# Ten ring slots and 17 expert places for the weight loads of a two-model transformer kernel, with all transfers issued by SyncE and ScalarE

## The reference, cut to what matters

```python
def first_block(x, c, ctx, ...):
    for i in range(2):
        mod_x = (silu(c) @ w_ada[i] + b_ada[i])          # "ada": 1024 x 6144
        hx = rms_norm(x) * (1 + sc1) + sh1
        zx = hx @ w_in[i]; mx = concat(attention, pool_mix, fourier_mix)
        x = x + ga1 * (mx @ w_out[i])
        x = x + ga2 * swiglu(fx, w_gate_up[i], w_down[i])
        # the same for ctx in layer 0
# second model: zx = h @ w_in_2 (attention q k v, mLSTM q k v o, gates), @ w_out_2,
# router over 32 experts, top 2 of one group; each expert: (silu(h @ w1) * (h @ w3)) @ w2
# final rms_norm with norm_f_g_2
```

## Time and profile before

| | before |
|---|---|
| median of 3 runs | 1637.65 us (1637.15 to 1637.92) |
| the profiled execution | 1636.89 us, span 1635.1 us |
| mean granted TensorE clock | 0.93 |
| busy: TensorE / VectorE / ScalarE / GpSimd | 87% / 39% / 32% / 5% of the span |
| DMA | 395 MB, mean 242 GB/s |
| chain that ended last | PE 67%, DMA 22% (of it `R<-in_w_dram` 20%, `R<-in_w_ada_dram` 1%) |
| 192 expert loads | 1024 KB each, median 23.0 us from issue to landing |

### The profile page before, as it was taken

The page is one execution under the profiler, slowest core; times in us unless marked ns, Lnnn a source line. Parts: engine busy times, 40 slices in busy tenths (PEclk is TensorE's granted clock), DMA queues, the critical chain, the costliest instruction groups (busy, mean ns, idle before and its releaser), DMA issues.

```text
span 1635.1 us, 24940 instructions
## 1 busy us (share of the span) xinstructions
PE 1427.8 (87%) x10475; PEld 1057.2 (65%) x10476; DVE 639.6 (39%) x1232; ACT 523.6 (32%) x975; POOL 74.2 (5%) x80
## 2 busy tenths in 40 slices
PE   5998999999999999989999999998886766677565
PEld 3654476888888886847999989898643333333232
DVE  3336445333333344565655666576421111110111
ACT  4425524322122324554544454564310000000001
POOL 2000022000000012002000010000000000000000
PEclk9999999999999999999999999999897787777777
DMA  9874952613421332766656447335899999999995
GB/s 361 338 267 169 283 195 88 190 53 122 154 65 56 97 108 100 282 204 212 216 179 210 143 173 233 97 110 200 346 417 417 418 417 417 418 418 417 417 417 238
DMA packets 165244, 395.06 MB, mean 242 GB/s; under 512 B 8244, under 2 KB 121448, under 8 KB 139272
## 3 DMA queue, kind: packets, MB, share of 16 engines
q1 hardware_dynamic: 163480, 390.56, 64.9%
q0 software_dynamic: 1216, 2.21, 0.4%
q10 hardware_dynamic: 432, 0.63, 0.1%
HBM read 392.32 MB, written 1.05 MB: 241 GB/s over the span
## 4 chain that ended last, share of the span: by engine, by line
PE 67%; DMA 22%; ACT 4%; DVE 4%; issue 2%; POOL 0%; SPq 0%; DVEq 0%; ACTq 0%; POOLq 0%
DMA R<-in_w_dram 20%; PE ps L901 14%; PE ps L907 14%; PE ps L902 14%; PE ps L2734 3%; PE ps L601 3%; PE ps L923 2%; PE ps L924 2%; PE ps L929 2%; PE ps L2783 2%; PE ps L2812 1%; PE ps L1217 1%; PE ps L1274 1%; DMA R<-in_w_ada_dram 1%; PE ps L1248 1%
## 5 line engine op out<-in xcount | busy, mean ns | idle before, releaser
L870 DVE TENSOR_TENSOR WL<-R,WH 128x1024 fp32r<-128x1024 f32 (+1 forms) x202 | 226.4, 1134 | 206.6 <-ACT WH L860 206.6
L2734 PE MATMUL ps<-R,XG 128*32 128x256 f32 x2048 | 180.8, 513 | 127.4 <-DMA R<-in_w_dram 120.5
L901 PE MATMUL ps<-HH,WH 128*128 128x256 f32 (+2 forms) x872 | 273.0, 335 | 0.3 <-ACT WH L860 0.3
L902 PE MATMUL ps<-HL,WH 128*128 128x256 f32 (+2 forms) x872 | 270.3, 330 | 0.0
L860 ACT ACTIVATE WH<-R 128x1024 fp32r<-128x1024 f32 (+1 forms) x202 | 191.2, 961 | 150.5 <-PE ps L907 113.2
L2734 PEld LDWEIGHTS ps<-R,XG 128*32 128x32 f32 x2048 | 90.4, 139 | 210.5 <-issue 196.0
L901 PEld LDWEIGHTS ps<-HH,WH 128*128 128x128 f32 (+1 forms) x872 | 164.3, 188 | 23.7 <-issue 6.5
L902 PEld LDWEIGHTS ps<-HL,WH 128*128 128x128 f32 (+1 forms) x872 | 164.9, 189 | 16.7
L907 PE MATMUL ps<-HH,WL 128*128 128x256 f32 (+2 forms) x872 | 164.7, 331 | 0.0
L901 PE MATMUL ps<-GH,WH 128*128 128x512 f32 (+1 forms) x480 | 153.7, 339 | 0.1
L902 PE MATMUL ps<-GL,WH 128*128 128x512 f32 (+1 forms) x480 | 153.5, 339 | 0.0
(11 more groups left out here) (494 smaller groups left out, 1739.8 us busy)
## 6 DMA issues: line engine op xcount, KB each, us to landing
R<-in_w_dram SPq DMA_DIRECT2D x192, 1024.0 KB, 23.0
R<-in_w_ada_dram SPq DMA_DIRECT2D x72, 1024.0 KB, 6.7
R<-in_w_gate_up_dram SPq DMA_DIRECT2D x40, 1024.0 KB, 7.5
R<-in_w_in_dram SPq DMA_DIRECT2D x20, 1024.0 KB, 9.2
R<-in_w_down_dram SPq DMA_DIRECT2D x16, 768.0 KB, 4.5
R<-in_w_down_dram SPq DMA_DIRECT2D x16, 640.0 KB, 4.4
R<-in_w_in_dram SPq DMA_DIRECT2D x8, 512.0 KB, 9.4
R<-in_w_out_dram SPq DMA_DIRECT2D x16, 256.0 KB, 4.3
```

Of the source, the lines that this page charges most:

```text
L870: last = e.tensor_tensor(L, w, H.bitcast(F32), ALU.subtract)
L901: e.matmul(b[0:n, 0:N], H[:, k, 0:n], xh(k, N), start=(k == 0), stop=False)
L902: e.matmul(b[0:n, 0:N], H[:, k, 0:n], xl(k, N), start=False, stop=False)
L2734: mm = e.matmul(PS[4][32 * g:32 * g + 32, 0:256], x[:, 4 * hf + k, :], w[g // 2][:, k, 256 * (g % 2):256 * (g % 2) + 256], start=(hf == 0 ...
```

## The change

The software queue's ring shrinks from 16 KB to 128 bytes, and GpSimd issues no transfers any more. The room gives the weight ring two slots more (`SLOTS` 10), behind the split buffers, and lets three expert places instead of two lie in the area of `WPF`, `SC` and the split buffers; there are 8 further places, of which one is used once, so 17 take part in the turn. SyncE issues what GpSimd issued, at fixed points of its load order; ScalarE issues `RES` at the start and `TWO` at the head of `act_second`.

```diff
-BASE = 16512
-SLOTS = 8
+SCRATCH = 128
+BASE = 128 + SCRATCH
+SLOTS = 10
...
+    def slot_at(k):
+        return oR + 8 * KB * k if k < 8 else oW + 22 * KB + 8 * KB * (k - 8)
+
+    R = [at(f"R{i}", [128, 2048], F32, slot_at(i)) for i in range(SLOTS)]
...
-    WR = at("WR", [128, 8, 36], F32, oZ + 16 * KB)
-    RB = at("RB", [128, 36], F32, oZ + 16 * KB + 1152)
+    WR = at("WR", [128, 8, 36], F32, o2 + 22240)
+    RB = at("RB", [128, 36], F32, o2 + 23392)
...
     def act_start(e):
+        e.dma_start(RES[:, 0:S_COS], A["k_res"][:, 0:S_COS]).then_inc(d_res, 16)
         load_vectors(e, 0)
...
+    def sp_rotary_table(e):
+        e.wait_ge(s_xt, 8)
+        e.dma_start(RES[:, S_COS:S_END], A["k_res"][:, S_COS:S_END]).then_inc(d_cs, 16)
+        e.wait_ge(s_init, 2)
+
+    def sp_mixer_weights(e, layer):
+        if layer:
             e.wait_ge(s_mx, 20)
...
+    def sp_positions(e):
         e.wait_ge(s_mx, 30)
...
+    def sp_router_weights(e):
         e.wait_ge(s_mm, first_of["in2"])
-        e.dma_start(TWO[:, :], A["k_two"]).then_inc(d_two, 16)
+        for c0, n, wn, bn in ((0, 4, "w_rg_2", "b_rg_2"), (4, 32, "w_re_2", "b_re_2")):
+            e.dma_start(WR[:, :, c0:c0 + n], A[wn][0].rearrange("(k p) n -> p k n", p=128)).then_inc(d_wr, 16)
+            e.dma_start(RB[:, c0:c0 + n], A[bn][0].partition_broadcast(128)).then_inc(d_wr, 16)
...
     def act_second(e):
         act_split(e, first_of["in2"] + 1)
+        e.wait_ge(s_mm, first_of["in2"])
+        e.dma_start(TWO[:, :], A["k_two"]).then_inc(d_two2, 16)
         act_rstd(e, 4, 256, 4)
...
-    MORE = ((o2 + 8320, (s_mld, 24)), (oW, (s_mm, N_TILES)), (oW + 8 * KB, (s_mm, N_TILES)), (oH + 8 * KB, (s_mm, N_TILES)),
+    MORE = ((o2 + 8320, (s_mld, 24)), *((oS + 6816 + 8 * KB * q, (s_mm, N_TILES)) for q in range(3)), (oH + 8 * KB, (s_mm, N_TILES)),
             (oG, (s_mm, N_TILES)), (oX, (s_rtp, 4)), (oX + 8 * KB, (s_rtp, 5)))
-    ONCE = 3
+    ONCE = 4
...
+    first_top = latest[SLOTS + 1]
...
+    def sp_final_gain(e):
         e.wait_ge(s_mm, N_TILES)
         e.dma_start(NFB[:, :], A["norm_f_g_2"].partition_broadcast(128)).then_inc(d_nf, 16)
...
             for load in ring.loads[2:]:
+                if load is ring.loads[16]:
+                    sp_rotary_table(e)
+                    sp_mixer_weights(e, 0)
+                elif load is tiles[first_of["gu", 0, 0] + 10].parts[0][0]:
+                    sp_mixer_weights(e, 1)
+                elif load is tiles[first_of["gu", 1, 0] + 10].parts[0][0]:
+                    sp_positions(e)
+                elif load is tiles[first_of["in2"] + 5].parts[0][0]:
+                    sp_router_weights(e)
+                elif load is first_top:
+                    sp_final_gain(e)
                 if load.fill is not None and load.after is not None:
                     e.wait_ge(*load.after.used)
```

More of the change, by code:

```diff
@@ L174, in block_program @@
     GL = at("GL", [128, HALF, 512], F32R, oG + 22 * KB)
-    R = [at(f"R{i}", [128, 2048], F32, oR + 8 * KB * i) for i in range(SLOTS)]
+    def slot_at(k):
+        return oR + 8 * KB * k if k < 8 else oW + 22 * KB + 8 * KB * (k - 8)
+    R = [at(f"R{i}", [128, 2048], F32, slot_at(i)) for i in range(SLOTS)]
     WH = [at(f"WH{i}", [128, HALF, 128], F32R, oW + i * 11264) for i in range(2)]
@@ L186, in block_program @@
     SG = at("SG", [128, 8, 2], F32, oS + 6528)
-    WPF = at("WPF", [128, 4, 128], F32, oS + 6592)
-    ST = at("ST", [128, 48], F32, oS + 8640)
-    EB = at("EB", [128, 8], F32, oS + 8832)
+    WPF = at("WPF", [128, 4, 128], F32, oS + 6816)
+    ST = at("ST", [128, 48], F32, oS + 6592)
+    EB = at("EB", [128, 8], F32, oS + 6784)
     SC = at("SC", [128, KT, 32], F32, oS + 8864)
@@ L281, in block_program @@
     d_ring = [sem(f"d_ring{k}") for k in range(SLOTS)]
-    d_cs = sem("d_cs")
+    d_cs, d_two2 = sem("d_cs"), sem("d_two2")
     d_res, d_vec, d_wp, d_two, d_wr, d_out = (sem(n) for n in ("d_res", "d_vec", "d_wp", "d_two", "d_wr", "d_out"))
@@ L798, in held @@
     def held(tag, load):
-        return [at(f"{tag}{x}", [128, 8, 128], F32R, oR + 8 * KB * load.slot + 4 * KB * y) for y, x in enumerate("HL")]
+        return [at(f"{tag}{x}", [128, 8, 128], F32R, slot_at(load.slot) + 4 * KB * y) for y, x in enumerate("HL")]
     OUT2_ROOMS = [held("WQ", fourth)] + [[at(f"WO{j}{x}", [128, 8, 128], F32R, oH + 8 * KB * j + 4 * KB * y)
@@ L1849, in pe_rotary2 @@
         e.wait_ge(s_evi, 20 + 4 + m + 1)
-        e.wait_ge(d_two, 80)
+        e.wait_ge(d_two2, 16)
         if m >= 2:
@@ L2352, in block_program @@
     GSB, PM = small(6, 4), small(N_BLOCKS)
-    TJ = at("TJ", [128, 2, N_EXTRA, 32], F32, oW + 16 * KB)
+    TJ = at("TJ", [128, 2, N_EXTRA, 32], F32, oZ + 16 * KB)
     iota = TWO[:, B_IOTA:B_IOTA + 256]
@@ L2432, in pool_router @@
         e.wait_ge(s_m2l, 8)
-        for c0, n, wn, bn in ((0, 4, "w_rg_2", "b_rg_2"), (4, 32, "w_re_2", "b_re_2")):
-            e.dma_start(WR[:, :, c0:c0 + n], A[wn][0].rearrange("(k p) n -> p k n", p=128)).then_inc(d_wr, 16)
-            e.dma_start(RB[:, c0:c0 + n], A[bn][0].partition_broadcast(128)).then_inc(d_wr, 16)
         e.memset(ZERO[:, :], 0.0).then_inc(s_zero, 1)
+    def sp_final_gain(e):
         e.wait_ge(s_mm, N_TILES)
@@ L3061, in _ @@
         def _(e):
-            pool_mixer_weights(e, 0)
             pool_norm(e, 0, lambda k: MOD[:, 0, k, 1:2])
-            pool_mixer_weights(e, 1)
             pool_sums(e, 1, 512)
@@ L3069, in _ @@
             pool_sums(e, 3, 256)
-            pool_second(e)
+            pool_sums(e, 4, 256)
             pool_squares_a(e)
@@ L3093, in _ @@
             e.wait_ge(d_wp, 256)
-            e.wait_ge(d_two, 80)
+            e.wait_ge(d_two, 64)
+            e.wait_ge(d_two2, 16)
             e.wait_ge(d_wr, 64)
@@ L3109 @@
     from concourse.bass_utils import run_bass_kernel_spmd as _run
-    nc = _bacc.Bacc("TRN2", target_bir_lowering=False, num_devices=1)
+    nc = _bacc.Bacc("TRN2", target_bir_lowering=False, num_devices=1, dynamic_dma_scratch_size=SCRATCH)
     arrays, args = {}, {}
```

2 lines of the change are left out of this document (removed).

## The result

The changed kernel takes 1617.37 us (median of 4 runs, 1617.06 to 1619.09), against 1637.4 (1636.16 to 1637.92) for the kernel before in the same comparison: a ratio of 0.9874, 95% interval 0.9855 to 0.9893, or 20.0 us. The forecast was 1626.7 with a range down to 1622.5. The direction was right.

A forecast was written before the change was run, and what follows sets the result against it. The prediction took the expert stage as bound by DMA, its 192 loads of 1 MB; A 1.5 + B 3.7 - D 0.3 + C 6.0 = 10.9 us, off 1637.65, gave 1626.7 us, range 1622.5 to 1631.5.

The forecast's parts named there:

- gain C: Refill at the expert stage's start: three more load places bring the end forward 6.0 us (floor 4.5, ceiling 7.6).
- 173 loads at 2.53 us: Expert stage after the 19th load: remaining loads keep the old interval, so 1175.0 becomes 1613.0, against 1619.0 before.
- Start (A): Kernel start: eight ada loads issued in one go, small transfers later; eighth lands 1.5 us earlier (0.9 to 1.9).
- The rival that the order buys nothing: Kernel start: the new load order gains nought, time 1628.2 us; chance 0.08.
- in2 stall (B): Second model's in2 stage: wait for `ka0` goes, 2.2 us idle plus 1.5 lower clock, 3.7 in all (2.2 to 4.0).
- Rival 2: in2 stage: `ka0` waits for the router weights' short rows, or another engine holds tile 5; 1630.4 us, chance 0.13.
- `TWO` on ScalarE (D): Second model's norm: issuing `TWO` before ScalarE's table load costs 0.3 us, nothing if hidden, 0.6 if not.
- Rival 1: Expert refill: the added places buy nothing and only lengthen the queue; 1632.7 us, chance 0.07.
- The steady rate: Expert stage: load interval taken as unchanged; its error, half a per cent of 446 us (2 us), partly in the range.
- the loads still come at 2.53 us: Expert stage, sign expected in the profile after: the interval between load landings stays as before.
- the prediction is wrong if the steady rate differs: Expert stage, stated sign of failure: a changed rate of the steady run of loads would refute the forecast.

## Why the prediction was right or wrong

The bound was right, and so was the reading of each stage. What failed is one sentence behind gain C: "173 loads at 2.53 us".

- **Start (A), 1.5 forecast, 0.7 seen.** The landing moved by 1.4 and, with the small transfers put first again, back by 1.5: as to the landing, this term is confirmed. (Part of it is the place again: from the first to the eighth ada landing it took 17.51 with eight slots at the old offset and 17.13 at the new one, both with the small transfers late.) In the profiled execution 0.7 of it went to a lower clock in the matmuls behind it, 3.11 us for the twelve instead of 1.86. The sum had no term for that; the clock went the other way at the end, 1.4 us better. How much of A reaches TensorE varies by execution: at 980 us the kernels with B and with C taken back, whose program is the same up to that stage, are 1.9 and 0.5 ahead of before, the changed kernel 0.7, and the two with eight slots 1.4 and 1.6. The rival that the order buys nothing (1628.2) is out by the landings. The new issuer shows no gain in the steady run, as far as the runs go: the interval is 2.533 with GpSimd's transfers in the kernel (before) and without them (eight slots, old offset). No run changed the issuer and left the order. Order and issuer are two things, and the forecast counted the order alone.
- **in2 stall (B), 3.7 forecast, 3.9 seen**, and 3.7 gone when it is taken back alone. `ka0` landed at 979.73 where the forecast had 983, so the cover in front of ScalarE's split was about 6 us and not 4. The router weights cost what was put on them: issued from 969.31 to 970.85, the last landed at 977.05, 7.7 after the first issue (forecast 7); their rows are of 16 and 128 bytes, not up to 144. Rival 2 (the stall moves, 0.13) did not happen here, but with eight slots it did, at 3.2 us, so it was a fair rival.
- **`TWO` on ScalarE (D), 0.3 forecast, 0 seen.** It is issued beside the split.
- **Three places (C), 6.0 forecast, 6.7 seen to the 19th load**, 7.2 when taken back alone (6.6 of it behind the experts' first matmul). The forecast put the 19th at 1175.0 less the 4.9 of A, B and D, 1170.1; it landed at 1169.44. (By its own figures the sum gives 5.8 and not 6.0 there, 1180.84 - 1175.0.) The loads before the 19th come at the faster rate too, some ten of them in a row from the ninth on, which is 0.3 of the difference by that count. The rest lies in where the account cuts: from `N_TILES`, 5.4 ahead, the refill is 6.0. Rival 1 is out: without the three places the hole and most of the 7 us are back.
- **The steady rate, 0 forecast, 5.0 seen.** This is the step that failed. It was not weighed as a gain at all: the range gave it half a per cent (2 us), and the measured change is 1.1%. The cause is in the diff, in its least conspicuous line: `BASE` falls from 16512 to 256, and with it the eight old ring slots and four of the further places move from 128 past a multiple of 256 to a multiple. The prediction says of the moves that they cost nothing, "same sizes, same engines", and never looked at where the transfers land. Four kernels show it from both sides (before, 128 higher, 2.498, after, 64 higher, 2.545, eight slots at both offsets 2.499 and 2.533).
- **The end, 0 forecast, 1.4 seen**, 0.8 of it in the last 32 matmuls, at 1.00 for 0.71 of the clock. It is of these two executions and no gain of the change that a run shows.
- **Sum:** 10.9 forecast + 5.0 (rate) + 1.4 (end) + 0.7 (C) + 0.1 (up to the experts) + 0.2 (B) + 0.3 (D) - 0.8 (A) = 17.8, the difference of the two profiled executions. The medians are 2.2 further apart, because before's profiled execution was 0.5 under its median and after's 1.7 over: scatter of the runs.

The list of what would show it said "the loads still come at 2.53 us" and "the prediction is wrong if the steady rate differs". It named the right place, but no rival was made of it. A term of 446 us in a sum of small gains deserved one: a per cent of it is 4.5 us, more than B.

## What to carry to other kernels

When a diff moves buffers, work out where each transfer's destination begins, modulo 256 bytes, before calling the move free; in this kernel, bound by loads for 446 us, that one number was worth 5 of the 18 us, and 7.5 when changed alone, more than any part of the change that was forecast. Extra buffers paid here where a load waited for its slot (3.7 us, at `ka0`) and where an idle DMA could be filled ahead of a full stretch (7.0 us, in the refill); they did not raise the rate of a stretch that was already full (2.498 with 14 places in the turn, 2.504 with 17). And a transfer put into a single in-order queue can hold up what stands behind it (3.2 us here), so give it to the queue only where there are enough slots behind it as cover.

## What the runs showed of the hardware

**Where a load lands matters.** The interval between landings of 1 MB loads (128 partitions, 8 KB each, in rows of 8 KB or, for `w2`, 4 KB) by the place where they begin, the median over the steady run, read from the traces:

| kernel | places on a multiple of 256 | places off it (bytes past it) |
|---|---|---|
| before | 2.445 (the one such place) | 2.49 to 2.525 (128, 32) |
| before, 128 higher | 2.44 to 2.468 (2.455 over all loads) | 2.476 to 2.509 (128, 160) |
| after | 2.43 to 2.468 | 2.476 to 2.517 (160, 128) |
| after, 64 higher | | 2.506 (all loads; 64, 192, 224) |
| all on multiples of 256 | 2.436 to 2.495 (2.453 over all loads) | |

That is 1.5 to 2% for these loads, 417 to 424 GB/s. For the `w_in` column blocks with their 1 KB rows it is more: from 990 to 1000 us the kernel before moves 354 GB/s and its shifted twin 383, 8% more; with everything 64 bytes off it is 344, in the changed kernel 378. The traces' records of single rows show what one costs. From before to before, 128 higher, the mean time of an 8 KB row (1210 to 1400 us) goes from 313.9 to 310.1 ns, of a 4 KB row from 162.7 to 159.0, and of a 1 KB row (990 to 1000 us) from 50.5 to 46.2: some 4 ns a row, whatever its length.

In the kernel before, the places 32 bytes past a multiple took no less than those 128 past (2.52 to 2.525 against 2.49 to 2.52). Only the place that is written was moved in these runs, not the one that is read, and why its start counts is not shown.

**TensorE's interval changed when the split buffers were moved.** At a granted clock of 1.00 and never idle, fp32r matmuls of 128 x 128 weights by 256 columns came every 119.9, 116.8 or 118.3 ns (1501, 1541, 1522 in 180 us), and those with 512 columns every 232.8, 232.8 or 228.3 ns, in the changed kernel and with the split buffers 192 and 224 bytes lower. The same 176 matmuls of `WL` by `HH` in layer 1 took, from the first start to the last, 61.32 us in the kernel before, the changed one and all eight others in which the split buffers lie at their old distance from the other tiles, at whatever `BASE`, and 59.62, 59.61 and 60.18 in the three in which that distance changed (split buffers 192, 192 and 224 bytes lower). It was worth 5 us in layer 1 with 192 bytes, and 7.7 us in layer 0 and 3.3 in layer 1 with 224. The rows of a single instruction scarcely show it. After, with the buffers 192 lower, and 32 lower still (ns min/median/max; first and last start):

```profile
L912 PE MATMUL ps<-HH,WL x176: 278/282/286, 876.0 to 937.3; 128*128 128x256 f32 x176
```
```profile
L912 PE MATMUL ps<-HH,WL x176: 277/279/281, 873.0 to 932.6; 128*128 128x256 f32 x176
```
```profile
L912 PE MATMUL ps<-HH,WL x176: 279/279/280, 866.0 to 926.2; 128*128 128x256 f32 x176
```

A count in a window without idle time shows it best.

**Open.** In the steady run of five of the kernels (the changed one among them) there are three or four single intervals of 3.7 to 4.1 us between landings; before, 128 bytes higher, the changed kernel, 64 higher, and the two eight-slot kernels of one set have three or four of 3.3 to 3.6, and the kernels with C and with A taken back have none above 3.3. The last of these has the same mean of 2.504 as the changed kernel, so they don't decide the rate. No cause was found, and it was not tested. The granted clock near 30, 142, 655 and 780 us and at the end differed between executions by enough to move the whole by 1 to 2 us each time; differences of that size between two single executions say nothing of the kernels.
